# Attention scores as two rounded products from stacked parts, with loads and stores dealt out over the rounds

## The chip, the cores and the metric

The kernel runs on one core of a Trainium2 chip. The metric is the device time of one execution in microseconds, lower is better. The names: TensorE (PE) multiplies matrices, VectorE (DVE), ScalarE (ACT) and GpSimd (POOL) work on tiles in SBUF and PSUM, SyncE (SP) issues most DMAs. Each runs its own instructions in order and waits on semaphores.

## The reference

One decoder layer for a prompt of 1024 tokens and 8 sample sequences of 4 tokens (1056 tokens in all), width 1024, f32. What matters here:

```python
mod = silu(c) @ w_ada + b_ada            # six parts: shift, scale, gate, twice
h = rms_norm(x, g_pre_mix) * (1 + sc_a) + sh_a
q, k, v, xl, yl, ga, gr = split(h @ w_in)
q, k = rope(q), rope(k)                  # 16 query heads, 4 key heads, 64 wide
s = q . k / 8, masked to the 128 previous positions
p = exp(s - m) / (sum + exp(sink - m)),  m = max(max(s), sink);  o_attn = p @ v
xc = conv4(xl);  a, u = gates(xc);  h_t = a_t * h_(t-1) + u_t;  o_lru = h * gelu(yl)
merged = sigmoid(ga) * (o_attn @ w_at) + sigmoid(gr) * (o_lru @ w_lr)
x = x + gate * rms_norm(merged @ w_out);  then a mixture of experts, 32 experts, top 2
```

## The kernel before

Matrix products of the projections are made from rounded parts: each f32 operand is split by ScalarE (a copy rounded to `fp32r`, "up") and VectorE (the rest, "low"), and `three` adds up*up, up*low and low*up. Normalised inputs lie in SBUF as `hp_up` and `hp_low`. The stages, by the times of the profile:

- 0 to 115 us: norms, the first two parts of the conditioning, keys and values.
- 115 to 199.6: eight chunks of queries (m = 2 to 9), each 3 x 24 rounded products of 352 columns; ScalarE copies from PSUM and swaps halves, VectorE rotates (`rope`). After each chunk SP stores one eighth of `hp_up` and `hp_low` to DRAM (`h_store`, L633), for the stage of branch products.
- 199.6 to 223.2: attention of the samples, between pieces of the first xl projection.
- 223.2 to 571: eight rounds (`pe_round`, `act_round`, `dve_round`). Round i does attention for prompt block i (eight units s of two heads) and beside it the recurrent branch: xl for channel chunk i, yl for chunk i-1, conv, gates, scan.
- 571 to the end: branch products and mix by groups of tokens, router, expert rounds, output.

A round has ten steps s. TensorE in step s: scores of unit s (two plain f32 products, out 128x256, from `qst`, where GpSimd has staged each head's queries beside zeros, against `kT`), then the projection halves that `halves_at(s)` lists (output o is one third of the tokens; o = 0 to 2 is xl, 3 to 5 yl, 6 to 11 gates; a half is 12 rounded products), then the transposes of the probabilities of unit s-1, then the product with the values of unit s-2. Before, the halves per step are 1, 2, 2, 1, 1, 1, 2, 2, and steps 8 and 9 have three gate outputs each. In round 0 there are no halves; in their place `slab(s)` multiplies a slab of the conditioning weights, for the feed-forward gate and its like (`wslab`, two halves of 512 KB, 64 products of 64 columns each slab).

VectorE in step s: `first` (mask, maximum with `nsink`), a step of the recurrence (`lru_step`), from s = 4 on a step of `conv`, `second` (divide by the sum), in odd steps the copy of transposed probabilities to `pT`. The scan of 1024 tokens is run at the end of step 3, so before `first(4)`. ScalarE in step s: exponentials of unit s, copies of finished projection outputs (`keep_outs`), activations of the recurrence (step 1: two over 1056 columns; step 2: a square root, which needs another table than the exponentials), in even steps the copy to `pT`, then the attention output of unit s-2 into `oT`. The order on each engine is written by hand.

SP in the rounds: `lg_weights(i)` when the last gate output of round i-1 is done, `o_store(i-1)`, `ol_store(i-2)`, then `xl_weights(i+1)` and `yl_weights(i)` as their buffers come free. All of SP's DMAs share one queue.

## Time and profile before

| | us |
|---|---|
| median of 3 runs | 1672.56 (1672.17 to 1677.83) |
| the profiled execution | 1672.81 |
| its span, first to last instruction | 1671.0 |

From the page: PE is busy 95% of the span, PEld (weight loads, beside PE) 69%, DVE 45%, ACT 37%, POOL 8%. Mean granted clock of TensorE 0.981 of full speed. The page's line of slices shows, for each fortieth of the span in tenths, what is busy:

```profile
PE   6999989999999989999999999988998999999997
DVE  3523467888888764454455456660000000000006
ACT  4535545666666553343544354411110111111113
POOL 0000011111111000000000030000000000000002
PEclk7999999999999999999999999999999999999999
DMA  9464571111111385373447554979999999999988
```

A slice is 41.8 us, so the eight rounds are slices 6 to 13. Times below are microseconds from the start of the span. A matmul's own duration contains the pipeline's fill, so the cost of one in a row of many is the distance between starts. A timeline row that merges several (x4) has their common duration. In a name like `ps<-kT,qst` the output stands first.

### The profile page before, as it was taken

What the parts mean: (1) busy time and instruction counts of PE and PEld (TensorE: products, weight loads), DVE (VectorE), ACT (ScalarE), POOL (GpSimd) and SP (SyncE); (2) the same over time, 40 slices, a digit from 0 to 9 for tenths busy, and PEclk for the clock granted to TensorE, in tenths of its full rate; (3) what the DMA queues carried; (4) which work ended last, traced back from release to release, by engine and by line L of the source; (5) the groups of instructions that cost most, each with busy time, mean ns of one, the idle gap of its engine ahead of it and who ended that gap; (6) DMA issues with size and microseconds to landing.
All of it is one profiled execution on the core that took longest, in us unless ns stands there. A gap on an engine that the chain in (4) does not pass through costs nothing. (4 is left out here: it accounts for less than half of the span.)

```text
span 1671.0 us, 27190 instructions
## 1 busy us (share of the span) xinstructions
PE 1593.2 (95%) x11089; PEld 1154.4 (69%) x11089; DVE 744.5 (45%) x1474; ACT 626.4 (37%) x1130; POOL 126.8 (8%) x218
## 2 busy tenths in 40 slices
PE   6999989999999989999999999988998999999997
PEld 2889967888888889999999989752333333333334
DVE  3523467888888764454455456660000000000006
ACT  4535545666666553343544354411110111111113
POOL 0000011111111000000000030000000000000002
PEclk7999999999999999999999999999999999999999
DMA  9464571111111385373447554979999999999988
GB/s 360 168 209 139 171 253 36 55 55 55 55 48 49 124 283 175 126 277 127 159 144 239 189 200 153 350 296 397 421 408 427 425 415 426 409 412 390 407 334 321
DMA packets 98866, 404.66 MB, mean 242 GB/s; under 512 B 13431, under 2 KB 42135, under 8 KB 85800
## 3 DMA queue, kind: packets, MB, share of 16 engines
q1 hardware_dynamic: 88816, 381.28, 59.9%
q0 software_dynamic: 6992, 17.78, 2.7%
q10 hardware_dynamic: 2936, 3.88, 0.8%
q8 instruction: 88, 1.44, 0.3%
q14 instruction: 34, 0.28, 0.1%
HBM read 364.83 MB, written 44.32 MB: 245 GB/s over the span
## 5 line engine op out<-in xcount | busy, mean ns | idle before, releaser
L1234 ACT ACTIVATE wup<-wraw 128x1024 fp32r<-128x1024 f32 x120 | 126.7, 1059 | 265.6 <-PE ps L2113 222.6
L1734 DVE TENSOR_TENSOR wlow<-wraw,wup 128x1024 fp32r<-128x1024 f32 x112 | 136.9, 1224 | 148.6 <-ACT wup L1234 148.0
L2113 PE MATMUL ps<-wg,xT 128*32 128x512 f32 (+2 forms) x1072 | 158.8, 621 | 11.1 <-DMA wg<-w_gate 10.3
L2113 PE MATMUL ps<-wd,aT 128*32 128x512 f32 (+2 forms) x1072 | 150.0, 596 | 6.2 <-DMA wd<-w_down 4.6
L2113 PE MATMUL ps<-wu,xT 128*32 128x512 f32 (+2 forms) x1072 | 148.6, 594 | 2.8 <-DMA wu<-w_up 2.8
L2113 PE MATMUL ps<-h_up,wup 128*128 128x384 f32 (+1 forms) x384 | 125.7, 327 | 3.4 <-DVE wlow L1734 3.4
L2113 PE MATMUL ps<-h_up,wlow 128*128 128x384 f32 (+1 forms) x384 | 124.5, 324 | 0.0
L2113 PE MATMUL ps<-h_low,wup 128*128 128x384 f32 (+1 forms) x384 | 124.5, 324 | 0.0
L2113 PEld LDWEIGHTS ps<-wd,aT 128*32 128x32 f32 (+2 forms) x1072 | 47.3, 117 | 105.6 <-issue 103.9
L2113 PEld LDWEIGHTS ps<-wg,xT 128*32 128x32 f32 (+2 forms) x1072 | 45.0, 120 | 107.5 <-issue 104.2
L2113 PE MATMUL ps<-hp_up,wA_up 128*128 128x352 f32 x312 | 107.6, 345 | 1.1 <-DVE hp_low L1488 1.1
L1184 ACT ACTIVATE pp<-pp,ngm 128x257 f32<-128x257 f32 x128 | 64.3, 504 | 117.3 <-DVE ngm L1616 116.6
L2113 PE MATMUL ps<-hp_up,wB_up 128*128 128x352 f32 x312 | 106.7, 342 | 1.6 <-ACT gB L1160 1.6
L2113 PEld LDWEIGHTS ps<-wu,xT 128*32 128x32 f32 (+2 forms) x1072 | 45.5, 117 | 90.4 <-issue 88.4
L2113 PE MATMUL ps<-hp_up,wB_low 128*128 128x352 f32 x312 | 101.2, 324 | 0.0
L2113 PE MATMUL ps<-hp_low,wB_up 128*128 128x352 f32 x312 | 101.2, 324 | 0.0
L2113 PE MATMUL ps<-hp_low,wA_up 128*128 128x352 f32 x312 | 101.2, 324 | 0.0
L2113 PE MATMUL ps<-hp_up,wA_low 128*128 128x352 f32 x312 | 101.1, 324 | 0.0
L1424 ACT ACTIVATE aT<-ps 128x512 f32<-128x512 f32 x20 | 11.9, 597 | 227.9 <-PE ps L2611 227.9
L2055 DVE TENSOR_TENSOR sgm<-sgm,ps 128x512 f32<-128x512 f32 x20 | 13.8, 688 | 169.6 <-ACT sgm L1416 169.6
L964 POOL COPY qst<-oT 64x128 f32<-64x128 f32 x128 | 57.0, 446 | 278.9 <-ACT oT L1213 274.5
L2113 PEld LDWEIGHTS ps<-h_up,wup 128*128 128x128 f32 x384 | 73.2, 191 | 4.6 <-issue 4.2
(416 smaller groups left out, 3227.7 us busy)
## 6 DMA issues: line engine op xcount, KB each, us to landing
wg<-w_gate SPq DMA_DIRECT2D x32, 2048.0 KB
wu<-w_up SPq DMA_DIRECT2D x32, 2048.0 KB, 15.6
wd<-w_down SPq DMA_DIRECT2D x32, 2048.0 KB, 13.7
wraw<-w_ga SPq DMA_DIRECT2D x24, 512.0 KB, 3.7
wraw<-w_gr SPq DMA_DIRECT2D x24, 512.0 KB, 3.8
wraw<-w_at SPq DMA_DIRECT2D x24, 512.0 KB, 3.5
wraw<-w_lr SPq DMA_DIRECT2D x24, 512.0 KB, 3.5
wraw<-w_out SPq DMA_DIRECT2D x24, 512.0 KB, 3.5
```

The costliest lines, as they stand in the source:

```text
L964: pool.tensor_copy(qst[half, u % 4, a, :], oT[half, u, i * P:(i + 1) * P]).then_inc(u_staged, 1)
L1184: ins = act.activation(pp[:, s % 2, a, :], pp[:, s % 2, a, :], ACT.Exp, bias=ngm[:, s % 2, a:a + 1], scale=-1.0, accum_out=sme[:, s % 2, a ...
L1234: act.activation(wup[n % UP][:, :, :], wraw[n % RAW][:, :, :], ACT.Copy).then_inc(w_rounded, 1)
L1424: act.activation(aT[:, :, :], ps[:, 6, :].rearrange("p (m c) -> p m c", c=P), ACT.Copy).then_inc(a_kept, 1)
L1734: V.tensor_tensor(low_part(n)[:, :, :], wraw[n % RAW][:, :, :], wup[n % UP][:, :, :].bitcast(F32), ALU.subtract).then_inc(w_split, 1)
L2055: V.tensor_tensor(sgm[:, :], sgm[:, :], ps[:, 2, :], ALU.mult).then_inc(ch_moe, 1)
L2113: return pe.matmul(out, lhsT, rhs, start=start, stop=stop, skip_group_check=True)
```

## The change

- Scores: keys and queries are rounded and split as the weights are (`round_query`, `split_query`, ten each with the keys), both parts are stored to DRAM (`k_dram`, `q_store`), and loaded back per round: `kst` holds a head's key part twice, in the upper and the lower 64 partitions, `qst` the query's two parts in the upper and the lower 64. So a product over 128 partitions gives (q_up + q_low) * k_part, and two rounded products give a head's scores. GpSimd's staging is gone.
- Block 0 does without the half of its columns that was masked; `masks` is one pair of 128 columns.
- `h_store` moves from the query stage (where `q_store` takes its place) into the rounds. The slabs move from round 0 to one per round, behind the halves of step 3, with their loads. The modulation made from them (`add_bias(1)`, `scale_mod(1)`) moves to step 6 of the last round.
- Attention outputs go to a small `oS`, whose reuse needs the store of the block before (`st_o`).
- The halves per step become 2, 2, 2, 1, 2, 1, 1, 1. The scan moves behind `first(4)` and ahead of `second(4)`, and the first conv step behind `second(4)`.

```diff
-        oT = at("oT", [P, KC, TOK], big)
+        oT, q_low = at("oT", [P, KC, TOK], big), at("q_low", [P, KC, TOK], big, F32R)
+        kst = [at(f"kst{i}", [P, 2, 4, 2 * P], w, F32R) for i, w in enumerate((big, big + 5 * D))]
+        qst = [at(f"qst{i}", [P, 4, 2, P], big + (2 + i) * D, F32R) for i in range(3)]
+        oS, oSs = at("oS", [P, KC, P], big + 7 * D), at("oSs", [P, KC, NS], big + 8 * D)
...
+        wslab = [at(f"wslab{i}", [P, 4, 4, SB], zone_k + i * 1024) for i in range(2)]
...
+        def kq_loaded(i, half):
+
+            return 96 * (i // 2) + 80 + 16 * half
...
-            return (((0, 0),), ((0, 1), (1, 0)), ((1, 1), (2, 0)), ((2, 1),), ((3, 0),), ((3, 1),), ((4, 0), (4, 1)), ((5, 0), (5, 1)),
+            return (((0, 0), (0, 1)), ((1, 0), (1, 1)), ((2, 0), (2, 1)), ((3, 0),), ((3, 1), (4, 0)), ((4, 1),), ((5, 0),), ((5, 1),),
...
+            def q_store(u):
+
+                sp.wait_ge(kq_split, u + 3)
+                sp.wait_ge(st_kq, kq_stored(u))
+                for part in range(2):
+                    for a in range(2):
+                        sp.dma_start(head_rows(q_dram, part)[:, u, a, :], head_rows(q_part(u, part), a)).then_inc(st_kq, 16)
...
-                h_store(m - 2)
+                if m == 2:
+                    sp.wait_ge(kq_split, 2)
+                    for part in range(2):
+                        sp.dma_start(k_dram[:, :, :].rearrange("d (p x) n -> d p x n", p=2)[:, :, part, :], k_part(part)).then_inc(st_kq, 16)
+                else:
+                    q_store(m - 3)
...
+                sp.dma_start(o_dram[:, :, i * P:(i + 1) * P], oS[:, :, :]).then_inc(st_o, 16)
...
+            def load_keys(i):
+
+                if i < BLKS:
+                    ge(sp, u_scores, KC * (i - 1))
+                    c0 = P if i == 0 else 0
+                    for half in range(2):
+                        for a in range(2):
+                            sp.dma_start(head_rows(kst[i % 2], half)[:, a, :, c0:2 * P].bitcast(F32),
+                                         head_rows(k_dram, a)[:, :, (i - 1) * P + c0:(i + 1) * P]).then_inc(ld_kq[i % 2], 16)
+
+            def load_queries(n):
+
+                if n < 2 * BLKS:
+                    i, u0 = n // 2, 4 * (n % 2)
+                    ge(sp, u_scores, 4 * (n - 3) + 4)
+                    if n % 2:
+                        sp.wait_ge(ld_kq[i % 2], kq_loaded(i, 0))
+                    sp.dma_start(qst[n % 3][:, :, :, :].bitcast(F32), q_dram[:, u0:u0 + 4, :, i * P:(i + 1) * P]).then_inc(ld_kq[i % 2], 16)
...
+            def slab_halves(i):
+
+                for n in (2 * KC + 2 * i, 2 * KC + 2 * i + 1):
+                    slab_half(n)
+
+            sp.wait_ge(s_dve, 6)
+            sp.wait_ge(st_kq, kq_stored(KC - 1))
+            load_keys(0)
+            load_queries(0)
+            q_store(KC - 1)
+            sp.wait_ge(st_side, 64)
             for p in range(2):
-                sp.dma_start(O["kws"][:, p], kcx[:, p, :, NT:P + NT]).then_inc(st_kws, 16)
-            slab_half(16)
-            slab_half(17)
-            sp.wait_ge(s_pe, 3)
-            sp.wait_ge(st_kws, 32)
-            slab_half(18)
-            sp.wait_ge(s_pe, 8)
-            slab_half(19)
+                sp.dma_start(O["kws"][:, p], kcx[:, p, :, NT:P + NT]).then_inc(st_side, 16)
+            sp.wait_ge(st_kq, kq_stored(KC))
+            load_queries(1)
+            slab_halves(0)
+            xl_weights(1)
             sp.wait_ge(s_dve, 12)
-            sp.dma_start(o_dram[:, :, SEQ:TOK], oT[:, :, SEQ:TOK]).then_inc(st_o, 16)
-            sp.wait_ge(st_h, 32 * KC)
-            xl_weights(1)
-            for n in range(20, N_LATER):
-                slab_half(n)
+            sp.dma_start(o_dram[:, :, SEQ:TOK], oSs[:, :, :]).then_inc(st_o, 16)
+            load_keys(1)
+            load_queries(2)
             for i in range(1, KC):
                 lg_weights(i)
+                load_queries(2 * i + 1)
+                load_keys(i + 1)
+                load_queries(2 * i + 2)
+                slab_halves(i)
+                h_store(i - 1)
+                if i + 1 == KC:
+                    h_store(i)
                 o_store(i - 1)
                 if i >= 2:
                     ol_store(i - 2)
                 xl_weights(i + 1)
                 yl_weights(i)
...
-            for i in range(BLKS):
-                for u in range(KC):
-                    pool.wait_ge(u_out, 8 * i + u + 1)
-                    for a in range(2):
-                        half = slice(HD * a, HD * a + HD)
-                        pool.tensor_copy(qst[half, u % 4, a, :], oT[half, u, i * P:(i + 1) * P]).then_inc(u_staged, 1)
...
+            def round_query(u):
+
+                act.wait_ge(rope_done, u + 3)
+                act.wait_ge(st_kq, kq_stored(u - 1 if u > 4 else 0))
+                act.activation(q_part(u, 0).bitcast(F32R), oT[:, u, 0:SEQ], ACT.Copy).then_inc(kq_rounded, 1)
...
+                    if s == SLAB_STEP:
+                        act.wait_ge(ada_done, PIECES + N_SLAB + 2 * i + 2)
+                        act.activation(modq[:, 1, SB * i:SB * (i + 1)], ps[:, 1, 0:SB], ACT.Copy).then_inc(ada_kept, 1)
...
-                        act.activation(oT[:, s - 2, bass.ds(i * P, P)], ps[:, 7, 0:P], ACT.Copy).then_inc(u_out, 1)
+                        if s == 2:
+                            act.wait_ge(st_o, 16 * (i + 1))
+                            act.wait_ge(st_kq, kq_stored(KC))
+                        act.activation(oS[:, s - 2, :], ps[:, 7, 0:P], ACT.Copy).then_inc(u_out, 1)
...
+            def split_query(u):
+
+                dve.wait_ge(kq_rounded, u + 3)
+                V.tensor_tensor(q_low[:, u, 0:SEQ], oT[:, u, 0:SEQ], q_part(u, 0), ALU.subtract).then_inc(kq_split, 1)
...
                     if not begin and s < KC:
                         lru_step(i, s)
-                    if 4 <= s < KC:
+                    if not begin and s == 4:
+                        lru_step(i, "scan")
+                    if 4 < s < KC or begin and s == 4:
                         conv(i, s)
                     if s < KC:
                         second(i, s)
+                    if not begin and s == 4:
+                        conv(i, s)
+                    if s == 6 and i + 1 == KC:
+                        dve.wait_ge(ada_kept, PIECES + KC + 1)
+                        c(add_bias(1))
+                        scale_mod(1)
                     if s == 1 and i >= 2:
                         split_pair(1, 5 + i)
                     if s == 3 and i == 0:
...
-                    if not begin and s == 3:
-                        lru_step(i, "scan")
 
             dve_round(0, True)
-            dve.wait_ge(ada_kept, PIECES + KC + 1)
-            c(add_bias(1))
-            scale_mod(1)
             for i in range(1, BLKS):
...
+            def slab(i):
+
+                pe.wait_ge(proj_kept, number(i, 1) + 1)
+                pe.wait_ge(ada_kept, PIECES + 1 + i)
                 for h in range(2):
-                    n = 2 * KC + 2 * s + h
-                    pe.wait_ge(ld_wada[n % 4], 16 * (n // 4 - 2 if n % 4 > 1 else n // 4 + 6))
+                    n = 2 * KC + 2 * i + h
+                    pe.wait_ge(ld_wada[h], 16 * (n // 2 + 2))
                     for k in range(4):
                         for j in range(4):
-                            ins = mm(ps[AM * j:AM * (j + 1), slab_bank(s), 0:SB], cE[:, 4 * h + k, :], wslab[n % 4][:, k, j, :],
+                            ins = mm(ps[AM * j:AM * (j + 1), 1, 0:SB], cE[:, 4 * h + k, :], wslab[h][:, k, j, :],
                                      (h, k) == (0, 0), (h, k) == (1, 3))
                     ins.then_inc(ada_done, 1)
 
...
+                blocks = (1,) if begin else (0, 1)
+                c0 = P * blocks[0]
                 for s in range(KC + 2):
                     if s < KC:
-
-                        pe.wait_ge(u_staged, 16 * i + 2 * s + 3)
+                        n = 2 * i + s // 4
+                        if s % 4 == 0:
+                            pe.wait_ge(ld_kq[i % 2], kq_loaded(i, s // 4))
                         ge(pe, u_negmax, 8 * i + s - 1)
                         for a in range(2):
-                            out = ps[:, 3 + s % 2, a * 2 * P:(a + 1) * 2 * P]
-                            ins = mm(out, qst[:, s % 4, a, :], kT[:, s // 4, bass.ds(i * P, 2 * P)], True, True)
+                            out = ps[:, 3 + s % 2, a * 2 * P + c0:(a + 1) * 2 * P]
+                            for part in range(2):
+                                ins = mm(out, qst[n % 3][:, s % 4, a, :], kst[i % 2][:, a, 2 * (s // 4) + part, c0:], part == 0, part == 1)
                         ins.then_inc(u_scores, 1)
-                    if s < KC:
-                        slab(s) if begin else outs(i, s)
+                    if s < KC and not begin:
+                        outs(i, s)
+                    if s == SLAB_STEP:
+                        slab(i)
```

## Rows read from the trace of the kernel before

**Rows 1.** Stages: length, busy time of PE, PEld, DVE, ACT, POOL; PEclk, DMA share, GB/s

```profile
115.00:199.60 84.60, 84.60 (x522) 81.11 (x520) 34.80 (x29) 47.86 (x57) 0.00 (x0) 1.00 0.45 152
...
223.20:261.80 38.60, 32.26 (x654) 22.89 (x653) 25.64 (x84) 18.89 (x63) 5.98 (x16) 0.96 0.57 190
...
306.00:350.10 44.10, 43.66 (x286) 38.27 (x285) 36.12 (x97) 27.52 (x67) 7.76 (x17) 1.00 0.16 52
...
526.50:571.00 44.50, 43.85 (x285) 38.06 (x283) 34.43 (x96) 27.28 (x66) 4.33 (x10) 1.00 0.12 40
```

**Rows 2.** TensorE's timeline in round 2: start, duration, operation; in brackets the idle before

```profile
318.68 0.60 PE L2329 MATMUL ps<-ident,pp 128*128 128x128 f32 x4
319.21 0.66 PE L2113 MATMUL ps<-pT,vtok 128*64 128x128 f32 x8
319.80 1.13 PE L2113 MATMUL ps<-kT,qst 128*128 128x256 f32 x4
...
320.93 0.32 PE L2113 MATMUL ps<-hp_low,wA_up 128*128 128x352 f32 x1
...
322.69 0.60 PE L2329 MATMUL ps<-ident,pp 128*128 128x128 f32 x4
...
344.07 0.66 PE L2329 MATMUL ps<-ident,pp 128*128 128x128 f32 x4
345.03 0.67 PE L2113 MATMUL ps<-pT,vtok 128*64 128x128 f32 x8 [0.31 <-ACT oT L1213]
```

**Rows 3.** TensorE's timeline in the value projection, rounded products of 256 columns

```profile
71.78 0.28 PE L2113 MATMUL ps<-wV_up,hp_up 128*128 128x256 f32 x1
...
72.97 0.29 PE L2113 MATMUL ps<-wV_low,hp_up 128*128 128x256 f32 x1
```

**Rows 4.** TensorE's timeline, a slab in round 0

```profile
224.16 1.10 PE L2113 MATMUL ps<-wslab,cE 128*32 128x64 f32 x64
```

**Rows 5.** ScalarE's timeline in round 2

```profile
314.03 1.26 ACT L1167 ACTIVATE gC<-gA,lcur 128x1056 f32<-128x1056 f32 x1
...
316.56 0.51 ACT L1184 ACTIVATE pp<-pp,ngm 128x257 f32<-128x257 f32 x1
...
318.02 1.28 ACT L1171 ACT_TABLE_LOAD   x1
319.31 1.08 ACT L1171 ACTIVATE xc<-xc 128x1056 f32<-128x1056 f32 x1
...
322.36 0.51 ACT L1184 ACTIVATE pp<-pp,ngm 128x257 f32<-128x257 f32 x1
```

**Rows 6.** VectorE's timeline in round 2

```profile
320.97 0.17 DVE L1614 COPY pp<-nsink 128x2 f32<-128x2 f32 x1 [1.21 <-PE ps L2113]
...
323.57 0.17 DVE L1625 RECIPROCAL rcp<-sme 128x2 f32<-128x2 f32 x1
...
324.90 2.28 DVE L1668 TENSOR_TENSOR_SCAN olst<-gC,xc 128x1024 f32<-128x1024 f32 x1
...
327.87 0.17 DVE L1614 COPY pp<-nsink 128x2 f32<-128x2 f32 x1
...
342.46 0.35 DVE L1627 TENSOR_SCALAR pp<-pp,rcp 128x256 f32<-128x256 f32 x1
```

**Rows 7.** VectorE's timeline, samples and round 0

```profile
209.17 0.57 DVE L1579 TENSOR_REDUCE mxs<-ps 128x3 f32<-128x396 f32 x1 [1.79 <-PE ps L2113]
...
226.47 0.17 DVE L1625 RECIPROCAL rcp<-sme 128x2 f32<-128x2 f32 x1 [1.14 <-ACT pp L1184]
```

**Rows 8.** Short stretches: length, PE busy, PEclk, DMA share, GB/s

```profile
228.00:232.00 4.00, 2.12 (x50) 1.00 0.95 338
252.00:254.00 2.00, 0.00 (x0) 1.00 0.00 0
256.00:257.00 1.00, 1.00 (x6) 0.50 0.00 0
261.80:266.00 4.20, 4.20 (x25) 1.00 0.66 212
```

More of the change, by code:

```diff
@@ L52 @@
 N_SLAB = 2 * KC
+SLAB_STEP = 3
 SB = D // 2 // KC
@@ L288, in build @@
         u0 = tmp0 + 1032 + 56
-        qst = at("qst", [P, 4, 2, P], u0)
         pp = at("pp", [P, 2, 2, 2 * P + 1], u0 + 1024)
-        pT = at("pT", [P, 2, 4, P], u0 + 1024 + 1024 + 32)
-        assert u0 + 3 * 1024 + 32 <= wv0 and u0 + 1024 <= tmp0 + 1056 + 1056
+        pT = at("pT", [P, 2, 2, 2, P], u0 + 1024 + 1024 + 32)
+        assert u0 + 3 * 1024 + 32 <= wv0
         l1 = ew0 + 2 * EW - 5 * TOK - 8
@@ L534, in lane_part, with k_part, q_part, kq_stored @@
             return ap[NS * lane:NS * (lane + 1), 0:FD].rearrange("r (h c) -> r h c", h=2)
+        def k_part(part):
+            return oT[:, 2 + 2 * part:4 + 2 * part, 0:SEQ]
+        def q_part(u, part):
+            return q_low[:, u, 0:SEQ].bitcast(F32) if part else oT[:, u + 3 if u < 5 else u - 2, 0:SEQ]
+        def kq_stored(units):
+            return 16 * 2 + 64 * units
+        def kq_loaded(i, half):
+            return 96 * (i // 2) + 80 + 16 * half
+        def head_rows(ap, a):
+            return ap[HD * a:HD * a + HD]
         def bc(ap, shape):
@@ L1116, in _ @@
                         round_pair((m + 1) % 2, (m + 1) // 2 + 1)
+                    if g == 1 and m > 2:
+                        round_query(m - 3)
                 swap(m, oT[:, m - 2, :])
+            round_query(KC - 1)
             def store_mod(g):
@@ L1179, in act_round @@
             def act_round(i, first=False):
+                c0 = P if first else 0
                 for s in range(KC + 2):
@@ L1562, in _ @@
                     split_pair(0, 2)
+            for p in range(2):
+                dve.wait_ge(kq_rounded, p + 1)
+                V.tensor_tensor(k_part(1)[:, p].bitcast(F32R), kT[:, p, P:P + SEQ], k_part(0)[:, p], ALU.subtract).then_inc(kq_split, 1)
+            def split_query(u):
+                dve.wait_ge(kq_rounded, u + 3)
+                V.tensor_tensor(q_low[:, u, 0:SEQ], oT[:, u, 0:SEQ], q_part(u, 0), ALU.subtract).then_inc(kq_split, 1)
             for m in range(2, 10):
                 split_pair((m + 1) % 2, (m + 1) // 2 + 1)
+                if m > 2:
+                    split_query(m - 3)
                 rope(m, oT[:, m - 2, :])
@@ L2229, in outs @@
                         pe.wait_ge(proj_kept, number(i, o) - 2)
+                    if (o, part) in ((1, 0), (4, 0)):
+                        pe.wait_ge(ada_kept, PIECES + 1 + i + (o == 4))
                     if (o, part) == (0, 0):
@@ L2326, in pe_round @@
                         for a in range(2):
-                            for hf in range(2):
+                            for hf in blocks:
                                 q = 2 * a + hf
@@ L2333, in pe_round @@
                         pe.wait_ge((u_kept, u_kept_a)[w], 4 * i + (s - 2) // 2 + 2)
-                        pe.wait_ge(u_out, 8 * i + s - 2 + 4)
-                        if begin and s == 2:
-                            pe.wait_ge(ada_kept, PIECES + 2)
+                        ge(pe, u_out, 8 * i + s - 2)
                         for a in range(2):
-                            for hf in range(2):
+                            for hf in blocks:
                                 v0 = (s - 2) // 4 * P + HD * a
                                 ins = mm(ps[HD * a:HD * a + HD, 7, 0:P], vtok[:, i + hf, v0:v0 + HD],
-                                         pT[:, w, 2 * a + hf, :], hf == 0, hf == 1)
+                                         pT[:, w, a, hf, :], hf == blocks[0], hf == 1)
                         ins.then_inc(u_pv, 1)
-                    if begin and s == KC:
-                        pe.wait_ge(ada_kept, PIECES + KC + 1)
                     if s >= KC:
@@ L2739, in constants @@
     out = np.float32(-1e30)
-    masks = np.zeros((P, BLKS, 2 * P), np.float32)
-    masks[:, :, :P] = np.where(k >= q, 0, out)[:, None, :]
-    masks[:, :, P:] = np.where(k <= q, 0, out)[:, None, :]
-    masks[:, 0, :P] = out
+    masks = np.zeros((P, 2 * P), np.float32)
+    masks[:, :P] = np.where(k >= q, 0, out)
+    masks[:, P:] = np.where(k <= q, 0, out)
     t, j = (m % NT)[:, None], np.arange(P + NT)[None, :]
```

115 lines of the change are left out of this document (54 added, 61 removed).

## The prediction

> **What bounds the kernel now.** I first read the table of stages [rows 1]: in each of the seven rounds between 261.8 and 571.0 us (the second and the last stand for them) TensorE is busy some 43.7 of 44.1 us, VectorE 36.12, ScalarE 27.52, the DMA engines 16%. So the rounds are bound by TensorE, with VectorE only 8 us behind. Round 0 is different: TensorE 32.26 of 38.6 us. Then I read one round (from 306.00) engine by engine, since the change shifts work inside it. TensorE's timeline [rows 2] has its only visible wait at 345.03 (0.31 us). A unit of attention costs: transposes 0.53 (318.68 to 319.21), values 0.59 (319.21 to 319.80), then scores and half a projection output 2.89 (319.80 to 322.69). The rounded products of 352 columns start 0.16 apart (320.93 to 322.69 is eleven of them), so a half output is 1.93 and the scores with their change of format 0.96. VectorE's timeline [rows 6] shows the slack: it ends the last unit's normalisation at 342.8 (342.46 and the 0.35 that it lasts), and TensorE comes for it at 344.07 [rows 2]. That is 1.3 us. By my reading this number decides the case.
>
> **The scores.** Two plain 128x256 products become four rounded ones. The nearest rows are the rounded products of 256 columns in the value projection: ten starts in 1.19 us, 0.12 each [rows 3]. So 0.48, and 0.14 for the switch of format (bounds 0.10 and 0.19, as the first rounded product after plain ones is now that much late inside the 0.96): 0.62 instead of 0.96, 0.34 less for each of 8 units, 2.7 us a round. With the lower price it is 3.0, and nothing is saved if the four products cost what the two did.
>
> **The slabs.** A slab of 64 small products takes 1.10 with its pipeline's tail, 1.0 without [rows 4]. Round 0 loses seven of them, each later round gains one: +1.0. TensorE's own work per round is then 44.1 - 2.7 + 1.0 - 0.3 (the wait at 345.03) = 42.1.
>
> **The order inside a round.** This is where I think the gain goes. `halves_at` puts two halves of xl in each of steps 0, 1 and 2 (before: 1, 2, 2), so the outputs that ScalarE must copy before its other work come later against a round that is meant to be shorter. I walk through one round, t from its first score product, durations from the rows throughout. TensorE: output 0 is done at 4.5, output 1 at 8.8, output 2 at 13.8 (0.62 or, with no switch of format in step 1, 0.48, and 3.86 per step; transposes 0.53 from step 1 on, values 0.59 from step 2 on). ScalarE has each 0.2 later (the 0.32 that a product lasts less the 0.16 to the next). So it copies output 1 at 9.0 to 9.35, then runs the two gate activations, 2.5 (314.03 to 316.56), to 11.9, then unit 2's exponentials, then waits and copies output 2 at 14.0 to 14.55. Only behind that copy come the table load, the root, a pT copy, an output copy and the table load back, 4.34 without a gap (318.02 to 322.36) [rows 5], and unit 3's exponentials begin at 18.9, where now they begin at 16.4. VectorE takes them up 1.2 later, at 20.1 (its wait of 1.14 for two exponentials, [rows 7]). From second(3) to the end of second(7) it has no gap now: 323.57 to 342.8, 19.2, and it holds the scan (2.97, 324.90 to 327.87), five normalisations, four maxima, four conv steps, two pT and a weight split [rows 6]. The change reorders that list and takes nothing from it. Some 0.2 goes with GpSimd's copies beside it. So the last normalisation ends at 20.1 + 19.0 = 39.1. TensorE would be there at 36.3: eight scores 4.8, twelve halves 23.2, slab 1.0, seven transposes 3.7, six values 3.6. It waits 2.8. From there to the next round is 6.0 now (344.07 to 350.1), of which 0.3 is the wait that goes, as ScalarE is then done with its copy: 5.7. The round is 39.1 + 5.7 = 44.8, against 44.1: +0.7, seven times, 4.9 us. The scan behind the maximum does release first(4) 3 us sooner, but the scan then stands ahead of second(4) and everything in VectorE's queue behind it, and VectorE's sum is unchanged. In the last round the modulation (two operations on 512 columns, at pT's rate some 0.7 each) takes the place of a weight split: +0.3.
>
> The table load is a place to weigh a page. The row has 1.28, and the root starts 1.29 behind the load's start [rows 5], so no pause follows. The Trainium skill (ScalarE: Activation LUTs, What ACT_TABLE_LOAD costs) puts 1283 ns and a drain of about 1380 ns on every switch. By the page, two switches on this chain would add 2.8 us to each round, some 19 us in all; by the row, nothing, and I go by the row.
>
> **Round 0.** VectorE and ScalarE alternate there, and a gap of 1.14 for the exponentials is open in each of the first units [rows 7]. Half the columns go. My estimate is a fixed part and about 1 ns a column, half of that for a scaling, from 0.51 for 257 columns of an exponential and 0.35 for 256 of a scaling [rows 5, 6]. That is 0.13 off each of two maxima, half of that off each of two scalings, 0.13 off each of two exponentials where they are open (first four units), 0.27 off pT: 0.65 for four units, 0.4 for four, 0.8 for three pT, and some 1.2 in which units waited behind slabs for their scores. About 6 us (bounds 4, if columns cost less than their share, and 8). Its seven slabs were hidden by this alternation and give nothing more.
>
> **What I put at nothing.** VectorE's ten splits and ScalarE's ten roundings (some 12 us each) lie mostly in the query stage, 115 to 199.6, where TensorE is busy for all of the 84.6 us, VectorE for 34.80 and ScalarE for 47.86 [rows 1]. The last split goes ahead of the samples' first maximum, where VectorE waits 1.79 for TensorE [rows 7]. Without that cover it would be 1.2. GpSimd's copies go; nothing waited for them but scores (below nothing: VectorE runs up to 0.3 a round slower beside them, and that is in my 19.0). SP: the keys, queries, two slab halves and two to four input stores now stand ahead of o_store, ol_store and the next weights in its queue. At 321 to 356 GB/s for fully busy engines (212/0.66, 338/0.95) [rows 8] the 4.9 MB up to and with o_store take 13.8 to 15.3 us and begin 2 us into the round. ScalarE now needs o_store done before it writes oS at t = 17.4, and behind it stand the table load and unit 3's exponentials. It lands at 16 to 17.4: just in time, no cost, but no margin either.
>
> **The sum** against the profiled execution (1672.81 us, span 1671.0; the median of the runs is 1672.56, so both are the same to 0.02%): -6.0 (round 0) + 4.9 (seven rounds) + 0.3 (the last) = -0.8, so 1672.
>
> **Rivals.** (a) TensorE stays the bound: ScalarE's chain is shorter than I walked, or VectorE catches up. For it: VectorE's busy time is only 36.1 of a round. Against: the gaps it has lie at the round's ends. Rounds of 42.1, -2.0 seven times, and -6: 1653. Half way between, 1662. (b) Slower, the store: if small pieces of 512 bytes (queries and o_store) move at half the rate of the rows, the burst is 3 to 5 us longer, o_store lands 3 us too late at t = 20, and the walk's chain shifts by that. It decides from 17.4 on, and each us costs 7: 3 us is 1672 + 21 = 1693. For it: the engines are idle now where it will be crowded, and no row has such a mix. (c) The change doesn't do what it says: rounded scores from separately loaded weights cost as much as plain ones. Then output 2 is 1.0 later and so is the chain: 1672 + 7 = 1679. Against it: [rows 3]. (d) The wait of 2.8 before the last transposes lowers the clock. In round 0 a pause of over 3 us around 252 to 254, with the clock at 1.00, was followed by a clock of 0.50 (1.2 GHz instead of 2.4) for some 3 us, of which 256 to 257 is one [rows 8]. If 2.8 is enough, each round loses 1.5, the half of those 3: 1682.
>
> **How the numbers follow.** My walk 0.5 (its own range 1664 to 1680, 1 us a round), (a) 0.25, (b) 0.12, (c) 0.05, (d) 0.08. The range is 1655 to 1689. A measurement of this kernel can tell about 0.5%, 8.4 us, from no change. Faster by more: (a) and the low edge of the walk, 0.28. Slower by more: (b), (d) and an edge, 0.24. Within: 0.48.
>
> **What would show it.** Rounds of 44 to 45 us in the new kernel, TensorE idle 2 to 3 us before each round's last transposes with VectorE as releaser, score groups 0.62 long, round 0 near 32.5 us, queries' stage still 84.6. If TensorE has no wait and the rounds are 42, (a). If ScalarE waits for a DMA ahead of the copy to oS, (b). A granted clock under 0.9 behind the waits is (d). A wait of the first scores for their keys (they land by my reading before 223) would be an error that no case here holds.

## The result, and the profile after

The changed kernel takes 1698.34 us (median of 4 runs, 1692.04 to 1699.41) against 1673.41 for the kernel before beside it: ratio 1.0139, 95% interval 1.0112 to 1.0167. It is 1.4% slower. I had forecast 1672, with 1655 to 1689 as the range.

The table of short stretches of the kernel after, with the columns of [rows 1], says where:

```profile
113.60:197.40 83.80, 83.80 (x520) 80.70 (x518) 42.57 (x36) 53.83 (x64) 0.00 (x0) 1.00 0.47 163
221.10:256.50 35.40, 22.67 (x158) 14.67 (x157) 19.78 (x83) 15.45 (x56) 0.00 (x0) 0.61 0.46 118
304.60:353.10 48.50, 43.51 (x350) 37.71 (x348) 35.73 (x97) 27.84 (x68) 0.00 (x0) 0.96 0.45 135
403.40:449.30 45.90, 41.91 (x350) 36.75 (x348) 35.83 (x97) 27.86 (x68) 0.00 (x0) 1.00 0.47 142
308.00:312.00 4.00, 4.00 (x29) 4.00 (x28) 3.08 (x10) 2.22 (x8) 0.00 (x0) 1.00 1.10 241
316.00:320.00 4.00, 4.00 (x32) 3.64 (x31) 3.28 (x6) 2.99 (x8) 0.00 (x0) 1.00 1.03 409
```

- The query stage (first line) is still TensorE without a gap. VectorE has 42.57 us there for 34.80, ScalarE 53.83 for 47.86: the splits are hidden.
- Round 0 (second line) is 3.2 us shorter, but at a granted clock of 0.61.
- Rounds 1 to 7 take 338.6 us where they took 309.2. That is +29.4 and the whole loss; everything else together gained some 3. Two of these rounds are in the table: round 2 (third line) and round 4 (fourth line), the shortest, the only one whose granted clock stays at 1.00.

Round 2 (the round of [rows 2, 5, 6]) tells how. TensorE's timeline, the products of attention and what stands beside them:

```profile
308.96 0.64 PE L2199 MATMUL ps<-kst,qst 128*128 128x256 f32 x4
313.28 0.60 PE L2422 MATMUL ps<-ident,pp 128*128 128x128 f32 x4
...
319.16 0.74 PE L2199 MATMUL ps<-kst,qst 128*128 128x256 f32 x4
321.74 1.10 PE L2199 MATMUL ps<-wslab,cE 128*32 128x64 f32 x64
...
324.57 0.66 PE L2199 MATMUL ps<-pT,vtok 128*64 128x128 f32 x8 [1.14 <-ACT oS L1283]
...
345.91 0.66 PE L2422 MATMUL ps<-ident,pp 128*128 128x128 f32 x4 [3.25 <-DVE pp L1709]
346.51 1.13 PE L2199 MATMUL ps<-pT,vtok 128*64 128x128 f32 x8
347.56 3.20 PE L2199 MATMUL ps<-xc,wlg 128*128 128x352 f32 x6
350.69 0.67 PE L2199 MATMUL ps<-pT,vtok 128*64 128x128 f32 x8
351.29 2.04 PE L2199 MATMUL ps<-xc,wlg 128*128 128x352 f32 x6
```

The scores did what was promised: 313.28 less 308.96, less two halves (3.86), is 0.46; 321.74 less 319.16, less one half (1.93), is 0.65 with the switch of format. But TensorE now waits 3.25 us for VectorE ahead of the last transposes, and behind the wait a gate output takes 3.20 where the next takes 2.04. Round 4 has the same wait without that:

```profile
443.68 0.66 PE L2422 MATMUL ps<-ident,pp 128*128 128x128 f32 x4 [3.25 <-DVE pp L1709]
444.28 0.66 PE L2199 MATMUL ps<-pT,vtok 128*64 128x128 f32 x8
444.88 2.04 PE L2199 MATMUL ps<-xc,wlg 128*128 128x352 f32 x6
```

The clock falls behind the wait in six of the seven rounds. ScalarE's timeline of round 2, and two lines of VectorE's:

```profile
318.78 1.28 ACT L1233 ACT_TABLE_LOAD   x1
320.07 1.09 ACT L1233 ACTIVATE xc<-xc 128x1056 f32<-128x1056 f32 x1
321.06 0.58 ACT L1276 ACTIVATE pT<-ps 128x512 f32<-128x512 f32 x1
324.15 0.28 ACT L1283 ACTIVATE oS<-ps 128x128 f32<-128x128 f32 x1 [2.51 <-issue]
324.44 1.28 ACT L1247 ACT_TABLE_LOAD   x1
```
```profile
326.94 0.17 DVE L1707 RECIPROCAL rcp<-sme 128x2 f32<-128x2 f32 x1 [3.87 <-ACT pp L1247]
...
345.50 0.35 DVE L1709 TENSOR_SCALAR pp<-pp,rcp 128x256 f32<-128x256 f32 x1
```

ScalarE stands 2.51 us before its first write to oS. The releaser reads "issue", that is, nothing the profile names; the code has two waits there, for o_store and for the stores of the queries, and SP itself waits for the latter ahead of round 0's second queries. In rounds 1 to 6 this is 2.06, 2.51, 3.07, 1.32, 2.25 and 2.50: 13.7 us. Round 7, where no next keys are loaded, has none. TensorE meets the delay in three places: 1.14 us for ScalarE's copy to oS (line of 324.57), 0.60 before the transposes of 337.60, and a longer last wait. SP's timeline and the list of DMA issues (KB, us from issue to landing) agree: o_store is issued at 311.63 and takes 12.4, to 324.0, which is 19.7 us behind the round's first scores (304.37).

```profile
305.26 0.38 SPq L741 DMA_DIRECT2D qst<-q_dram  x1
305.68 2.56 SPq L731 DMA_DIRECT2D kst<-k_dram  x4
308.29 0.60 SPq L741 DMA_DIRECT2D qst<-q_dram  x1
308.93 1.51 SPq L653 DMA_DIRECT2D wslab<-w_ada  x2
...
311.63 0.56 SPq L722 DMA_DIRECT2D o_dram<-oS  x1
```
```profile
o_dram<-oS SPq DMA_DIRECT2D x1, 512.0 KB, 12.4
```

While queries and keys move the DMA engines are full at 241 GB/s; later they carry 409 (last two lines of the table). The rates in 40 slices of 0.35 us from 305.2 on:

```profile
GB/s 0 59 199 201 195 297 297 341 323 307 260 225 214 219 196 217 249 237 219 208 199 200 201 208 263 291 300 325 347 367 445 386 433 386 364 441 398 398 422 409
```

The slow stretch is 13 slices of 196 to 249 GB/s, 4.6 us in all.

### The profile page after: what moved, and what is told of

It is laid out like the page before. It is cut to its first block and busy times, and to the rows that moved or that the text cites. A ratio compares the mean times of both kernels' runs of the same rounds, so it can differ in the third digit from the quotient of the medians.

```text
span 1697.1 us, 27072 instructions
## 1 busy us (share of the span) xinstructions
PE 1579.4 (93%) x11041; PEld 1142.0 (67%) x11041; DVE 749.1 (44%) x1484; ACT 635.2 (37%) x1140; POOL 68.3 (4%) x87
## 5 line engine op out<-in xcount | busy, mean ns | idle before, releaser
L2199 PE MATMUL ps<-wg,xT 128*32 128x512 f32 (+2 forms) x1072 | 154.8, 604 | 10.6 <-DMA wg<-w_gate 9.7
L2199 PE MATMUL ps<-hp_up,wA_up 128*128 128x352 f32 x312 | 102.2, 327 | 1.0 <-DVE hp_low L1556 1.0
L1247 ACT ACTIVATE pp<-pp,ngm 128x257 f32<-128x257 f32 (+1 forms) x128 | 62.5, 490 | 107.8 <-DVE ngm L1698 107.7
L2199 PE MATMUL ps<-hp_up,wB_up 128*128 128x352 f32 x312 | 100.8, 323 | 1.6 <-ACT gB L1222 1.6
L2141 DVE TENSOR_TENSOR sgm<-sgm,ps 128x512 f32<-128x512 f32 x20 | 13.8, 688 | 165.1 <-ACT sgm L1484 165.1
L2422 PE MATMUL ps<-ident,pp 128*128 128x128 f32 x240 | 41.3, 295 | 38.1 <-DVE pp L1709 38.1
## 6 DMA issues: line engine op xcount, KB each, us to landing
wd<-w_down SPq DMA_DIRECT2D x32, 2048.0 KB, 14.1
```

What stands on the lines that cost most here:

```text
L1247: ins = act.activation(pp[:, s % 2, a, c0:], pp[:, s % 2, a, c0:], ACT.Exp, bias=ngm[:, s % 2, a:a + 1], scale=-1.0, accum_out=sme[:, s % ...
L2141: V.tensor_tensor(sgm[:, :], sgm[:, :], ps[:, 2, :], ALU.mult).then_inc(ch_moe, 1)
L2199: return pe.matmul(out, lhsT, rhs, start=start, stop=stop, skip_group_check=True)
L2422: ins = pe.transpose(ps[:, 5 + w, q * P:(q + 1) * P], pp[:, w, a, hf * P:(hf + 1) * P], ident[:, :])
```

## The experiments

All stand beside runs of the kernel before (medians 1672.31 to 1675.01). "Store wait" is ScalarE's wait at oS summed over rounds 1 to 6, "stall" TensorE's wait ahead of the last transposes. The lengths of rounds, waits and stalls come from the one profiled execution of each kernel.

**1. The store alone.** e1_store_first:

```diff
                 lg_weights(i)
+                o_store(i - 1)
                 load_queries(2 * i + 1)
...
                     h_store(i)
-                o_store(i - 1)
```

> The store of the last block's attention outputs goes ahead of the keys, queries, slabs and input stores in SP's queue. If the late store costs what ScalarE waits for it (2.1, 2.5, 3.1, 1.3, 2.3, 2.5 us in six rounds), the waits vanish and the kernel gains 12 to 14 us: 1685. If the crowded queue costs in another way (the waits are cover for something else that is late, such as weights), it gains under 4 us: 1694 to 1698. The wait before the last transposes (3.25 us in a round) and the low clock behind it should stay, since the order of the steps is unchanged.

Measured: 1673.25 us, ratio 1.0013 (0.9991 to 1.0035). Its round from 301.60, the end of that round on TensorE, and o_store's landing:

```profile
301.60:345.90 44.30, 41.63 (x350) 36.90 (x349) 35.77 (x97) 28.01 (x69) 0.00 (x0) 1.00 0.51 147
```
```profile
340.05 0.66 PE L2422 MATMUL ps<-ident,pp 128*128 128x128 f32 x4 [2.67 <-DVE pp L1709]
340.65 0.66 PE L2199 MATMUL ps<-pT,vtok 128*64 128x128 f32 x8
341.24 2.04 PE L2199 MATMUL ps<-xc,wlg 128*128 128x352 f32 x6
```
```profile
o_dram<-oS SPq DMA_DIRECT2D x1, 512.0 KB, 4.5
```

No store wait is left, and five of seven rounds are 44.3 or 44.4 us long: my walk had 44.8. The late store was worth 25 us by the medians (23 by rounds 1 to 7 of the two traces), nearly twice the 13.7 that ScalarE waited and more than I expected. What doubled it is in the last line: after a stall of 2.67 the gates run at full clock, where I had expected stall and clock to stay as they were. The stalls are 2.67 to 2.98 in six rounds (the clock fell in one of them, behind 2.84) and 3.10 in the last (it fell).

**2. The clock alone.** e3_warm puts twelve identity products, whose results are not used, ahead of the round's last transposes:

```diff
+                    if s == KC and not begin:
+                        pe.wait_ge(u_negmax, 8 * i + KC - 1)
+                        for _ in range(12):
+                            mm(ps[:, 3, 0:P], ident[:, :], ident[:, :], True, True)
                     if 1 <= s <= KC:
```

> Twelve plain 128x128 products of the identity into a free bank, 2.6 us, are put into TensorE's wait before a round's last transposes (rounds 1 to 7). They change no result and nothing waits for them that does not wait already. If the low clock behind that wait costs what the tails of the rounds show (7.2 to 8.7 us instead of 5.7, about 13 us in all), the clock stays at 1.00 there and the kernel gains 10 to 13 us: 1686 to 1688. If the long tails have another cause, the time stays at 1698.

Measured: 1684.13 us, ratio 1.0081 (1.0055 to 1.0107).

```profile
337.30 2.94 PE L2199 MATMUL ps<-ident 128*128 128x128 f32 x24
340.62 0.66 PE L2426 MATMUL ps<-ident,pp 128*128 128x128 f32 x4 [0.38 <-DVE pp L1709]
341.22 0.66 PE L2199 MATMUL ps<-pT,vtok 128*64 128x128 f32 x8
341.81 2.04 PE L2199 MATMUL ps<-xc,wlg 128*128 128x352 f32 x6
```

The work before the transposes ends when it did, the store wait is still 14.1 us, and the clock stays at 1.00 in all seven rounds. The clock that fell behind the stall is 13 us of the changed kernel's time by the traces (rounds 1 to 7 take 325.4 us for 338.6), 14 by the medians and 10 by the ratios. Less its own store wait, each of rounds 1 to 6 is here 44.4 or 44.5 us long, with waits from 1.9 to 2.9: once the clock stays, a round grows by what ScalarE waits.

**3. Does the stall's length decide?** e11_store_late is e1 with one VectorE operation more ahead of the last normalisation:

```diff
                 dve.wait_ge(u_exp, 8 * i + s + 3)
+                if s == 7 and i:
+                    u(V.tensor_scalar(pp[:, w, 0, c0:2 * P], pp[:, w, 0, c0:2 * P], 1.0, None, ALU.mult))
```

> o_store first (1673, rounds of 44.3 us, stall ahead of the last transposes 2.67 to 2.98 us), with one more VectorE operation of some 0.35 us between unit 7's exponentials and its normalisation (a scaling by 1.0, which changes no value), so that the stall is 3.0 to 3.35 us with nothing else changed. If a slightly longer stall is what makes the clock fall (store and clock are coupled): the granted clock falls in most rounds as in the changed kernel, and each costs 0.4 + 2: 1686 to 1692. If the clock fell in the changed kernel for another reason than the stall's length: only 7 x 0.4 more, 1675 to 1677.

Measured: 1690.37 us, ratio 1.0086 (1.0066 to 1.0106).

```profile
344.01 1.11 PE L2424 MATMUL ps<-ident,pp 128*128 128x128 f32 x4 [3.17 <-DVE pp L1711]
345.05 1.13 PE L2201 MATMUL ps<-pT,vtok 128*64 128x128 f32 x8
346.11 3.89 PE L2201 MATMUL ps<-xc,wlg 128*128 128x352 f32 x6
```

An operation of 0.35 us cost 17 us by the medians (16 by the rounds of the traces, 12 by the ratios). The stalls are 2.92 to 3.43, the clock falls in every round, and rounds are 46.1 to 47.8 us. So store and clock are one cost: the late store adds some 0.4 us to a stall behind which the clock otherwise stayed up in most rounds. The length alone does not settle a round: the clock stayed behind 3.25 in round 4 of the changed kernel and fell behind 2.84 in one round of e1 and 2.92 in one of e11.

**4. The order of halves.** e2_halves_back is the changed kernel with the order of before; e4_store_halves has it and o_store first:

```diff
-            return (((0, 0), (0, 1)), ((1, 0), (1, 1)), ((2, 0), (2, 1)), ((3, 0),), ((3, 1), (4, 0)), ((4, 1),), ((5, 0),), ((5, 1),),
+            return (((0, 0),), ((0, 1), (1, 0)), ((1, 1), (2, 0)), ((2, 1),), ((3, 0),), ((3, 1),), ((4, 0), (4, 1)), ((5, 0), (5, 1)),
```

> Only the list of projection halves per step is that of the kernel before (1, 2, 2, 1, 1, 1, 2, 2). If the order costs by itself, as walked (the third xl output keeps ScalarE from its root), this gains 5 us: 1693. If the store decides when ScalarE goes on, the earlier output only lengthens its wait for the store by about 1 to 2 us and the kernel stays within 2 us: 1696 to 1700.

> Both edits, the store first and the halves back. By store (14), order (5) and, since VectorE is then done about when TensorE comes for the last unit, the clock (13): 1666 to 1670, rounds of 42.5 to 44. If the clock does not follow the wait, 1680. If moved work on VectorE (the scan ahead of the division of unit 4) is what makes TensorE wait, the wait before the last transposes stays at over 2 us and the time at 1680 to 1685.

Measured: e2 1684.95, ratio 1.0073 (1.005 to 1.0096); e4 1659.08, ratio 0.992 (0.99 to 0.9941). Both are faster than I expected, e2 by 8 us and e4 by 7. The first is a wait moved, not removed: ScalarE comes to oS earlier and waits 4.0 to 5.8 us. Then TensorE waits for ScalarE in the middle of the round, and the clock falls there in four of the seven rounds. The stall at the round's end is 0.8 us or less. The line of the wait, then two stretches around it (columns of [rows 1]):

```profile
324.27 1.13 PE L2199 MATMUL ps<-pT,vtok 128*64 128x128 f32 x8 [3.23 <-ACT oS L1283]
```
```profile
322.00:324.00 2.00, 0.00 (x0) 0.00 (x0) 0.00 (x0) 0.15 (x1) 0.00 (x0) 0.88 0.99 395
324.00:326.00 2.00, 1.73 (x11) 1.43 (x12) 0.00 (x0) 1.97 (x5) 0.00 (x0) 0.50 0.08 31
```

The second has neither wait. Its round:

```profile
299.30:342.30 43.00, 41.84 (x351) 36.99 (x349) 35.59 (x97) 27.91 (x69) 0.00 (x0) 1.00 0.51 152
```

TensorE is busy 41.84 of 43.0 us at full clock, and what it still waits for is mostly a slab's weights, 5.5 us over all rounds. This is the rounded scores' gain nearly as rival (a) had it: rounds 1 to 6 take 42.4 to 43.7 us, where (a) had 42.1.

**5. The scan's place.** e6_scan_back runs the scan at the end of step 3 again, and e8_store_halves_scan does so on e4:

```diff
-                    if not begin and s == 4:
-                        lru_step(i, "scan")
-                    if 4 < s < KC or begin and s == 4:
+                    if 4 <= s < KC:
                         conv(i, s)
...
-                    if not begin and s == 4:
-                        conv(i, s)
...
+                    if not begin and s == 3:
+                        lru_step(i, "scan")
```

> The changed kernel with the scan back at the end of step 3 (behind the pT copy, ahead of step 4's work) and the conv step of step 4 ahead of unit 4's normalisation, as before the change; all else as changed (1698). My walk: VectorE's list between unit 3's exponentials and the last normalisation has the same sum in either order, so the stall ahead of the last transposes stays at 3.2 us, ScalarE still waits 1.3 to 3.1 us for o_store, and the time is 1695 to 1701. Rival, the scan is what stretches the chain: it stands ahead of unit 4's division and lets ScalarE idle; with it back the last normalisation ends 0.5 to 1 us sooner, the stall is below 3 us, part of the clock loss goes too: 1685 to 1692. Rival on the other side: the move had helped, since unit 4's exponentials start 3 us sooner with the scan behind them; taken back, each round grows by 0.5 to 1 us: 1702 to 1706.

> o_store first and the order of halves of before (1659 together), with the scan back at the end of step 3. TensorE is there busy for 41.8 of 42.8 us a round. By my reading VectorE now has 1 to 2 us of slack behind its last normalisation, so the scan's place moves nothing: 1657 to 1661. Rival: the scan's later place is what gives VectorE that slack; taken back, TensorE waits again up to 1 us ahead of the last transposes: 1662 to 1666.

Measured: 1696.49 (ratio 1.0131, 1.0114 to 1.0148) and 1663.45 (0.9925, 0.9908 to 0.9943). On the changed kernel it moves nothing: its rounds are 48.5 us either way (the stall is 3.0 for 3.25, with the clock falling in every round). On e4 the ratios to the kernel before overlap; the traces have rounds of 43.5 for 43.0, with stalls of 0.2 to 1.2 us where e4 has one, so the later place may be worth 0.5 us a round once TensorE is the bound. The medians are too near to call that shown.

**6. Why the transfers are slow.** o_store waits behind queries and keys. Three layouts in DRAM were tried on the changed kernel: queries in pieces of 4 KB (e7_q_layout), keys too, each block stored twice (e10_kq_layout), and both as one block a load (e14_dense); and one order, lower and upper half in turn (e13_key_order). The edits of a load:

```diff
-q_dram[:, u0:u0 + 4, :, i * P:(i + 1) * P]
+q_dram[:, i, u0:u0 + 4, :, :]            # e7, e10
+q_dram[i, n % 2, :, :, :, :]             # e14
...
-head_rows(k_dram, a)[:, :, (i - 1) * P + c0:(i + 1) * P]
+head_rows(k_dram, a)[:, i, :, c0:2 * P]                  # e10
+k_dram[i, HD * a:HD * a + HD, :, c0:2 * P]               # e14
...
-                    for half in range(2):
-                        for a in range(2):
+                    for a in range(2):
+                        for half in range(2):            # e13
```

> The changed kernel with the queries laid out block by block in DRAM, so that a load of four units is contiguous pieces of 4 KB a partition instead of eight of 512 bytes; the stores of the queries (in the query stage, hidden) are then cut into pieces of 512 bytes instead. The keys keep their pieces of 1 KB. In the changed kernel the burst at a round's start ran at 205 to 241 GB/s while queries and keys moved and at 286 to 429 after. If the 512-byte pieces set that rate: 1.05 MB of queries take some 2 us less (at 350 to 400 GB/s instead of 220), o_store lands 2 us sooner, ScalarE's wait for it falls from 1.3 to 3.1 us to under 1, the stall ahead of the last transposes from 3.25 to under 3, and the clock stays up in most rounds: 1672 to 1685. If the keys' pieces or the writes among them set it, the wait for o_store stays above 1.3 us: 1694 to 1700.

> The changed kernel with queries and keys laid out block by block in DRAM (the keys with each block twice, once as the earlier and once as the present one): every load of them is now in contiguous pieces of 4 KB a partition; the stores in the query stage are in pieces of 512 bytes. With the queries alone (1697, o_dram landing 12.2 us behind its issue for 12.4) the slow stretch stayed: 930 transfers in 4 us at 228 GB/s, which are the keys' pieces of 1 KB. If the keys' pieces set the rate, 1.05 MB of them take 2.6 us at 400 GB/s for 4.6 at 228: o_store lands 2 us sooner or more, ScalarE's wait for it (12.9 us in six rounds) falls below 4, the stall ahead of the last transposes goes from 3.25 to 2.9, and part of the clock loss goes: 1672 to 1685. If the rate is set by something else about the keys (64 partitions a transfer, the writes), the waits stay: 1694 to 1700.

> The changed kernel with the four key loads of a round in another order: lower and upper half of the partitions in turn, where before two loads into the lower half stood ahead of two into the upper. Pieces and bytes are the same. If the key loads are slow because two in a row go to the same 64 partitions, o_store lands 1 to 2 us sooner: 1680 to 1690. If their pieces of 1 KB set the rate: 1694 to 1700.

> The changed kernel with queries and keys laid out in DRAM so that each load of them reads one contiguous block (512 KB of queries, 256 KB of keys), as each load of weights does. With pieces of 4 KB that lay 64 KB and 32 KB apart the slow stretch stayed (213 to 229 GB/s at full share, wait for o_store 10.0 us in six rounds, 1696). If the distance of the pieces sets the rate: the stretch runs at 350 to 400 GB/s, o_store lands 3 us sooner, ScalarE does not wait for it, the stall is 2.7 to 3.0 us: 1672 to 1680, as with o_store first. If not, the waits of 10 to 13 us stay: 1694 to 1700, and the cause of the slow stretch is none of what the layout decides.

| | us | ratio (interval) | store wait |
|---|---|---|---|
| e7 | 1696.79 | 1.0128 (1.0111 to 1.0144) | 12.9 |
| e10 | 1695.73 | 1.0134 (1.011 to 1.0159) | 10.0 |
| e13 | 1696.49 | 1.0136 (1.0115 to 1.0157) | 11.2 |
| e14 | 1694.41 | 1.013 (1.011 to 1.015) | 6.9 |

None removes the wait, and the time stays: all four intervals overlap that of the changed kernel. The pieces have a share, though: with one block a load the store wait is half (6.9 for 13.7). And e14 narrows the rest. Its rates in 40 slices of 0.29 us from 306.5 on:

```profile
DMA  0001795898978995999999999999998999999999
GB/s 0 0 0 36 224 339 171 299 399 299 370 285 313 370 214 128 271 299 214 214 256 228 228 228 228 199 228 228 228 256 342 385 428 428 413 385 399 428 456 399
```

The first queries come at some 300; then for 15 slices (4.3 us) the rate is mostly 228 or less, which moves about 1 MB, and the keys are 1.05. So the slow stretch is as long as before (4.6 us); what is quicker is what follows it, 342 to 428 GB/s at once, where the changed kernel takes six slices from 263 to 367. What only the key loads have is that each writes 64 of the 128 partitions. e17_keys_wide stores the keys twice and lets each load write all 128, with pieces of 1 KB again. The edit of the loads:

```diff
-                    for half in range(2):
-                        for a in range(2):
-                            sp.dma_start(head_rows(kst[i % 2], half)[:, a, :, c0:2 * P].bitcast(F32),
-                                         head_rows(k_dram, a)[:, :, (i - 1) * P + c0:(i + 1) * P]).then_inc(ld_kq[i % 2], 16)
+                    for a in range(2):
+                        for x in (0, 2):
+                            sp.dma_start(kst[i % 2][:, a, x:x + 2, c0:2 * P].bitcast(F32),
+                                         k_dram[a, :, x:x + 2, (i - 1) * P + c0:(i + 1) * P]).then_inc(ld_kq[i % 2], 16)
```

> The changed kernel with the keys stored twice in DRAM, so that each of the four key loads of a round writes 128 partitions (two pieces of 1 KB each) where before it wrote 64 (four pieces of 1 KB each); pieces and bytes are as in the changed kernel. If 64 partitions a load set the rate of 205 to 241 GB/s: the stretch of the keys runs at 300 GB/s or more and is 1.2 to 2 us shorter, ScalarE's wait for o_store (13.7 us in six rounds) falls below 5: 1680 to 1690, the less so as a stall above 3 us keeps the clock down. If not, the wait stays above 10 us and the time is 1694 to 1700: then no layout of the loads explains the rate.

Its rates in 40 slices of 0.35 us from 314 on:

```profile
GB/s 15 228 259 257 298 320 317 258 320 313 266 316 345 342 380 373 367 348 339 323 306 339 348 380 398 421 398 410 449 395 398 386 398 410 447 370 366 334 328 325
```

The trough is gone: after the first slices 257 GB/s and more throughout, where the changed kernel has 196 to 249 for 4.6 us. The store wait is 3.4 us (3.9 with round 7). So the width of the key loads is the cause of the slow stretch. The Trainium skill states it (SBUF — State Buffer, Door 1: The DMA port swizzle): partitions 0 to 63 reach only half of the DMA ports into SBUF, and a load to them measured 196 GB/s at 1 MiB for 328 on all 128. The traces agree in kind, with 228 GB/s in e14 for 257 to 345 in e17. The prediction priced the burst without it.

The time did not follow: 1698.48 us, ratio 1.014 (1.0123 to 1.0157), outside what I expected. The rounds are only 0.6 us shorter (47.9 for 48.5), because the stall stays at 3.09 to 3.49 and the clock now falls ahead of the last transposes in every round; at the same granted clock (0.93) the comparison is 47.8 for 50.3 and 49.6, rounds 3 and 5 of the changed kernel. And the eight key stores stand in SP's queue ahead of a projection's weights in the query stage, which starts round 1 8.7 us later. One line of TensorE there, where the changed kernel has no wait:

```profile
145.16 0.66 PE L2202 MATMUL ps<-hp_up,wB_up 128*128 128x352 f32 x1 [4.09 <-DVE wB_low L1551]
```

On e4 the wider loads are e18_best_wide:

> o_store first and the order of halves of before (1659), with the key loads on 128 partitions as in e17. If that speeds the burst, the 5.5 us of waits for slab weights shrink: 1654 to 1657. If not: 1657 to 1662.

1661.34, ratio 0.9913 (0.9894 to 0.9932). The waits for slab weights are gone and the rounds are 42.0 us, the 42.1 that I gave as TensorE's own work, but the query stage gives it back. The layouts of e7, e10 and e14 on e4 (e9_store_halves_q, e12_best_kq, e15_best_dense) came out at 1658.74, 1663.1 and 1662.2, ratios 0.9897, 0.9928 and 0.9929 for e4's 0.992: no gain that can be told from none.

**7. Round 0.** e16_warm_round0 has six identity products ahead of each unit's transposes in round 0 alone; e19_best_warm0 is that on e4:

```diff
+                    if begin and 1 <= s <= KC:
+                        pe.wait_ge(u_negmax, s)
+                        for _ in range(6):
+                            mm(ps[:, 3 + (s - 1) % 2, 0:P], ident[:, :], ident[:, :], True, True)
                     if 1 <= s <= KC:
```

> The changed kernel with six plain 128x128 identity products ahead of each unit's transposes in round 0 alone, in a bank that is free by then; their results are not used. Round 0 takes 35.4 us in the changed kernel (38.6 before; the prediction had 32.6), at a granted clock of 0.61. If the clock is what is missing: the granted clock in round 0 is above 0.8, the round takes 32.5 to 34 and the time falls by 1.5 to 3 us, to 1695 to 1697 (a difference that the trace shows better than the time). If round 0 is set by VectorE and ScalarE whatever the clock is: 35 to 36.5 us, and 1698 to 1700.

> o_store first and the order of halves of before (1659), with the identity products of e16 in round 0. There they took the granted clock of round 0 from 0.61 to 1.00 and the round from 35.2 to 31.6 us. If the three are independent: 3 to 4 us off 1659, 1655 to 1656. If the later rounds give it back (they are bound by TensorE with 0.5 us of slack on VectorE): 1658 to 1660.

Measured: e16 1694.34 (ratio 1.0137, 1.0117 to 1.0157), its round 0:

```profile
221.50:253.10 31.60, 26.67 (x254) 21.10 (x252) 19.78 (x83) 15.11 (x56) 0.00 (x0) 1.00 0.52 123
```

31.6 us for 35.4, VectorE's 19.78 the same: the lower clock cost 3.8 us. That is shown by the trace alone; the ratio is the changed kernel's (1.0139) within its interval. e19 is 1656.47 us, ratio 0.99 (0.9883 to 0.9916), the fastest here by its median, though its interval and e4's overlap: with the two repairs and this one, the change is 1.0% faster than before instead of 1.4% slower.

## Why the prediction was wrong

- **The scores** (0.62, or 0.48 with no switch of format; measured 0.65 and 0.46), **the slab** (1.10 with its tail), the query stage (83.8 us for my 84.6) and **the table loads** were right: 1.29 from load to root again, without the drain that the Trainium skill (ScalarE: Activation LUTs, What ACT_TABLE_LOAD costs) had.
- **The order inside a round** was right in its mechanism and 0.5 us a round too dear. The walk gave rounds of 44.8 with a stall of 2.8; with the store out of the way they are 44.3 with 2.67 to 2.98. Even in round 2 of the changed kernel ScalarE comes to oS at t = 17.3 (the walk: 17.4), VectorE takes up unit 3 at 22.6 (20.1) and ends the last unit at 41.5 (39.1): both are late by about the store wait of 2.51, and the 19 us between them are the walk's. That is where the gain of faster scores goes, as e4 shows from the other side (43.0).
- **The store** is the term that failed first. It was put at nothing: "It lands at 16 to 17.4: just in time" used 321 to 356 GB/s from [rows 8]. The burst began sooner than assumed, 0.9 us into the round for 2, but took 18.8 us for 13.8 to 15.3: it ran at 196 to 249 GB/s for 4.6 us of it, and o_store landed 19.7 us into the round. Rival (b) came true, but mostly for another reason than its small pieces of 512 bytes: with 4 KB in their place (e7) the store wait is 12.9 us for 13.7, while e17 shows the width. That each key load writes half of the partitions was to be seen in the diff (`head_rows(kst[i % 2], half)`).
- **The clock** is the second. I put "2.8 lowers the clock" down as rival (d) at 8%, apart from (b). They are not exclusive: the late store makes the stall 3.25, and with it (d) comes true in six of seven rounds. At 2.8 alone, as (d) had it, e1 shows the clock fall in one round of six. I added neither the pair's price, some 13.7 + 13.2, nor its chance.
- The sum of rounds 1 to 7, +29.4 in all, splits by e3's trace, where the clock stays up: clock 13.2 (325.4 us for 338.6), e3's store waits 14.1, and 2.1 for the order and the last round (325.4 less 14.1 is 311.3, for 309.2 before). My sum had 5.2 for these last and nothing for the other two.
- **Round 0** gave 3.2 for 6. TensorE is idle there for 12.7 of 35.4 us, where it was for 6.3 of 38.6, and its clock is 0.61 for 0.96. Half the columns went, but so did seven of the eight slabs, each 1.0 to 1.1 us of products. The prediction said that they were hidden and "give nothing more"; that they had kept the clock up is likely, but no run puts them back. At full clock (e16) the round gave 7.
- Round 0 begins 2.1 us sooner than before (221.1 for 223.2). That says nothing of the change: in traces of e1, e2, e3, e4, e6, e8, e11 and e13, whose code is that of the changed kernel up to there, it begins anywhere from 219.8 to 222.6. Why the clock falls behind one stall and holds behind another of the same length stays open; that it does is observed, no more.

## What to carry to other kernels

Where TensorE already stands some 3 us, price a further delay with the clock that it may cost (0.35 us a round cost 16 to 17 us over seven rounds here), and count two rivals that feed each other as one case. Take the price of a burst from transfers of the same shape on the SBUF side; partitions written count as much as bytes. And a late buffer is cheaply mended by the order in the issuing queue: o_store first was worth 25 us, while the wider key loads, the edit that sped up the burst most, started round 1 8.7 us later for their extra stores.

## What the runs showed of the hardware

- Loads to 64 partitions ran at 196 to 249 GB/s with the DMA engines full in pieces of 1 KB and mostly at 228 or less in one block (e14); the same bytes to 128 ran at 257 to 345 (e17).
- Behind the stalls of 3.01 to 3.50 us ahead of the last transposes TensorE dropped to 1.2 GHz in 59 of 62 rounds (the changed kernel, e1, e6, e7, e10, e11, e13, e14, e16 and e17), behind those of 2.67 to 2.98 in 3 of 8 (e1, e7, e11). In the changed kernel the loss was 1.2 to 1.9 us on the next gate output and up to 1 us on transposes and values around it.
- A stall of 3.25 us recurs to 0.01 us in rounds 1 to 6 of the changed kernel, whether the store wait of the round was 1.32 or 3.07, and still in e17 with 0.33. The rest of the lateness TensorE meets earlier in the round, in its waits for oS (5.6 us over the rounds) and before the transposes of step 6 (0.6 to 0.7 each).
